# Constant matrix products in TensorE's waits at three stage borders

## The reference

```
xn     = rmsnorm(x) * (1 + sc1) + sh1;  proj = xn @ w_in
o_a    = rwkv7(proj[...])               # 8 heads, matrix state
o_b    = mamba2(proj[...])              # 16 heads, SSD state
merged = g_a * (o_a @ w_pa) + g_b * (o_b @ w_pb)
x      = x + gt1 * (merged @ w_out)
xn2    = rmsnorm(x) * (1 + sc2) + sh2
x      = x + gt2 * peer(xn2)            # product keys, top 16, 16384 experts
y      = rmsnorm(x) * (1 + scf) + shf
```

## Time and profile before

| | us |
|---|---|
| median of 3 runs | 4293.69 |
| lowest and highest | 4291.61, 4294.74 |
| the profiled execution | 4287.3 |
| its span, first to last instruction | 4285.7 |

### The profile page before, as it was taken

One profiled execution on the slowest core, in us unless ns is written; L12 is line 12 of the kernel. 1 busy time (PEld: TensorE's weight loads), 2 busy tenths in 40 slices (PEclk: granted clock), 3 DMA queues, 4 the chain that ended last, 5 costly groups with the idle time before them and its releaser, 6 DMA issues. The chain is left out here.

```text
span 4285.7 us, 85292 instructions
## 1 busy us (share of the span) xinstructions
PE 4061.5 (95%) x32204; PEld 3709.4 (87%) x32204; DVE 3228.8 (75%) x6232; ACT 1438.3 (34%) x2563; POOL 1309.1 (31%) x1006
## 2 busy tenths in 40 slices
PE   8999999998669979999999997999999999999998
PEld 5998888887539869788888887999999999999998
DVE  5721425444853358899998997999999999999998
ACT  4212222121653222233358883222222222222223
POOL 5333231000012200144443333344443443434441
PEclk9999999999879999999999998999999999999999
DMA  6764674564643311144435668999999999999995
GB/s 219 229 205 177 228 243 159 217 222 153 160 156 106 125 56 35 57 145 143 144 125 201 224 216 314 303 299 300 304 300 299 301 300 303 300 299 299 301 303 197
DMA packets 532589, 928.61 MB, mean 217 GB/s; under 512 B 286848, under 2 KB 355200, under 8 KB 524816
## 3 DMA queue, kind: packets, MB, share of 16 engines
q1 hardware_dynamic: 396512, 549.91, 39.7%
q0 software_dynamic: 81056, 346.96, 24.2%
q10 hardware_dynamic: 54816, 28.85, 2.4%
HBM read 786.05 MB, written 206.30 MB: 232 GB/s over the span
## 5 line engine op out<-in xcount | busy, mean ns | idle before, releaser
L3586 POOL DMA_INDIRECT ex_rows<-expert_rows,ex_here x512 | 589.9, 1152 | 951.0 <-DVE acc_tok L3826 860.1
L3826 DVE SCALAR_TENSOR_TENSOR acc_tok<-ex_rows,ex_wsp,acc_tok 128x1024 f32<-128x1024 f32 x512 | 633.6, 1278 | 0.0
L2852 PE MATMUL ex_psa<-x_dense_high,eg_u_high 128*128 128x288 f32 x2048 | 604.7, 295 | 6.6 <-DVEq L3940 6.5
L2852 PE MATMUL ex_psa<-x_dense_low,eg_u_high 128*128 128x288 f32 x2048 | 604.7, 295 | 0.0
L2852 PE MATMUL ex_psa<-x_dense_high,eg_u_low 128*128 128x288 f32 x2048 | 604.5, 295 | 0.0
L2944 POOL TENSOR_TENSOR eg_u_low<-eg_u,eg_u_high 128x1024 fp32r<-128x1024 f32 x130 | 328.2, 2525 | 743.0 <-ACT eg_u_high L2939 743.0
L3705 ACT ACTIVATE ex_w<-ex_psa 128x288 f32<-128x288 f32 x256 | 105.4, 412 | 1059.4 <-PE ex_psa L2852 1059.4
L3618 PE MATMUL ex_pso<-ex_w_high,ex_v_high 128*128 128x288 f32 x2048 | 442.2, 298 | 17.9 <-DVE acc L3808 14.4
L3618 PE MATMUL ex_pso<-ex_w_high,ex_v_low 128*128 128x288 f32 x2048 | 440.2, 297 | 0.0
L3618 PE MATMUL ex_pso<-ex_w_low,ex_v_high 128*128 128x288 f32 x2048 | 438.9, 296 | 0.0
L3808 DVE TENSOR_TENSOR acc<-ex_pso,acc 128x576 f32<-128x576 f32 x512 | 373.7, 750 | 44.4 <-PE ex_pso L3618 44.4
(11 more groups left out here) (539 smaller groups left out, 9046.4 us busy)
## 6 DMA issues: line engine op xcount, KB each, us to landing
eg_u<-in_u SPq DMA_DIRECT2D x256, 512.0 KB, 5.4
expert_rows<-in_v SPq DMA_DIRECT2D x128, 512.0 KB, 6.9
ex_v<-in_v SPq DMA_DIRECT2D x128, 512.0 KB, 6.2
weights<-wt_stage SPq DMA_DIRECT2D x36, 1024.0 KB, 4.9
ex_g<-weights SPq DMA_DIRECT2D x128, 288.0 KB, 6.7
expert_rows<-eg_act SPq DMA_DIRECT2D x256, 128.0 KB, 1.7
proj<-in_out POOLq DMA_DIRECT2D x50, 548.5 KB, 6.2
in_w<-in_w_in SPq DMA_DIRECT2D x50, 512.0 KB, 5.1
```

Source lines behind the costliest of these rows:

```text
L2852: yield nc.tensor.matmul(out[:, 0:b - a], w[:, kc, :], half[:, kc, a:b], start=n == 0, stop=n == len(passes) - 1)
L3586: pool.indirect_dma_start(rows[i][:, :], None, table, index(here[par][:, t, j:j + 1]), element_offset=ROW_RUNS[t][0]).then_inc(s_row[i], 16)
L3826: v.scalar_tensor_tensor(out=acc_tok[:, t, :], in0=rows[i][:, at:at + D], scalar=wsp[:, i:i + 1], in1=acc_tok[:, t, :], op0=ALU.mult, op1= ...
```

## The change

A new helper issues products of the matrix of ones with a column of ones, broadcast to the width wanted, into a PSUM bank that nobody reads at that time. It increments no semaphore. It is called in five places: at the end of the sample stage (12 products of 512 columns, behind a wait for the fourth s_cp), at the start of the merge (6 of 288), at its end (12 of 288), at the start of the scores behind the first scaled tile (10 of 512), and at the end of the spread (24 of 128, into the bank of iota).

```
+def keep_array_busy(k, bank, count, width=512):
+    for _ in range(count):
+        k.nc.tensor.matmul(bank[:, 0:width], k.ones[:, :], bc(k.ones[:, 0:1], [P, width]), start=True, stop=True)
...
                 states(6)
                 states(7)
+                pe.wait_ge(s_cp, NPAIR)
+                keep_array_busy(k, ps_ce3[:, 2, :], 12)
...
+                keep_array_busy(k, pf[1], 6, TOK_CHUNKS_BANKED[0][1])
                 for m in range(KC):
                     h = m % 2
...
                     mm = nc.tensor.matmul(pf[0][:, a:b], k.ones[:, :], total[:, a:b], start=True, stop=True)
                 mm.then_inc(s_sum, 1)
+                keep_array_busy(k, pf[1], 12, TOK_CHUNKS_BANKED[0][1])
...
             @block.tensor
             def _(pe):
+                pe.wait_ge(NR.sem, NR.done("scaled", 0))
+                keep_array_busy(k, flat(pss[:, :, :]), 10)
                 for i in range(NQ):
...
                 in_line(body)
+                keep_array_busy(k, iota, 24, NK)
```

## The result

The changed kernel took 4297.95 us, the median of 15 runs (4292.70 to 4304.20); the kernel before, beside it, 4291.39 us, also of 15 (4284.59 to 4298.84). That is 6.6 us more; the ratio is 1.0016 with a 95% interval of 1.0008 to 1.0023. The forecast was 4301.8, within 4297 to 4307, and +8.1 us: the time is inside the range, though only 1 us above its lower end, and the change costs time but less than the 0.2% that I had named as the bound. The absolute forecast stood on a median of three runs of the kernel before (4293.69); on the 4291.39 of the 15 it would have been 4299.5.

The account below looks back on a forecast made before the run. The prediction had TensorE busy for 95% of the span, with only 13 us of half clock at three borders in reach. Its terms, 5.4 + 0 + 2.5 + 0 + 0.2 = +8.1 us, gave 4301.8 us, range 4297 to 4307.

Parts of the forecast that it names:

- What a constant product costs: Every constant product: 4 cycles a column, so 512 columns take 0.853 us at full clock and 1.707 at half.
- A: End of the sample stage: 12 products of 512 outlast SyncE's drain; +5.4 us, bounds 4.4 and 6.1.
- E: End of the spread: 24 products of 128 end about when SyncE's drain does; +0.2 us (0 to 0.4).
- C: End of the merge: 12 products of 288 outlast ScalarE's drain; +2.5 us, bounds 2.2 and 3.2.
- That constant products lift the clock: At the start of a run the clock stays low for 4.7 us, within 3.9 to 5.9, then rises.
- third rival: Products of a constant do not lift the clock, to be seen in A: about +30 us, 4324; chance 0.05.
- B: Start of the merge: 6 products of 288 take 2.9 us inside TensorE's 3.3 us wait; cost 0.
- D: Start of the scores: 10 products of 512 delay the first real product, but VectorE's pace hides this; cost 0.
- The gains: Faster starts of merge, scores and expert loop are hidden by ob_rounded, VectorE's pace and transfers; gain 0.
- first rival: Slow starts at the borders were on the path, so gains of 6.5 us reach the end: 4295.3 us; chance 0.07.
- second rival: At the borders the barrier is passed while constant products still stream: 4293.7 us, no change; chance 0.06.
- The sum: Whole kernel: 5.4 + 0 + 2.5 + 0 + 0.2 = +8.1 us, for 4301.8 us.

Follow-up runs that it names:

- e3: Changed kernel with only B, D and E, without A and C: 4288.08 us, ratio 0.9992 to the kernel before.
- e7: Changed kernel with only B and D, enlarged to 24 products of 288 and 20 of 512: 4302.65 us, timed once.
- e10: Changed kernel with only B and D, at 12 products of 288 and 14 of 512: 4294.48 us, timed once.
- e1: Changed kernel with only A, the other four calls out: 4294.93 us against 4291.62 for the kernel before, ratio 1.0011.
- e4: Changed kernel with only A, doubled to 24 products of 512: 4304.46 us, ratio 1.0031 to the kernel before.
- e6: Changed kernel, same places and counts, both operands of the constant products read as F32R: 4289.94 us against 4290.54 for the kernel before, ratio 0.9998.
- e8: Kernel before plus nine products of 288 ahead of the merge's output product and seven ahead of the norm sum: 4287.32 us against 4290.54, ratio 0.9993.
- e9: As e8 but eight products ahead of the output product: 4282.10 us against 4290.56 for the kernel before, ratio 0.9984.
- e12: The kernel of e9 again, unaltered: 4282.69 us against 4290.89 for the kernel before, ratio 0.9981.
- e2: Changed kernel with only C, the other four calls out: 4291.15 us, ratio 1.0000 to the kernel before.

## Why the prediction was right, point by point

**What a constant product costs: right.** 0.86 us for 512 columns at full clock (A doubled), 0.23 for 128 (24 took 5.5 us in E; worked out: 0.24), 0.50 for 288 (12 took 6.03 us in C; worked out: 0.48). One of the two supports was loose: the 512-wide records of the earlier trace rows differ by 0.47 us, not by the 0.43 of half of 2 x 512 columns / 1.2 GHz. The norm sum carried the figure.

**That constant products lift the clock: right.** The third rival (they don't, +30 us) is refuted by the clock of 0.93 and 1.00 in A, and by the first group of the merge in e3, where nothing but B's products ran ahead of it. But the rise came later than my bounds: in A it came about 6.4 us after the start of the run (1270.26 to some 1276.7, from 5 us at 0.93), where I had taken 4.7 with 3.9 to 5.9. At other places it came sooner: 4.3 to 4.6 us after the start of B in e3, e7 and e10, and 3.5 to 3.6 after that of D in e3 and e7, but 6.1 in e10.

**A: the right mechanism, mis-sized.** Forecast +5.4 within 4.4 to 6.1, measured 6.65, 6.67 and, with A alone, 3.78. The term was off by 1.3 us in the changed kernel: 0.9 from the later rise, and 0.4 because 12 products take 10.6 us at full clock where I had 10.24. The bound below was missed because the clock at the start of the run is not fixed: at high clock TensorE's own last products also end a microsecond earlier, which I had left out. That the total fell into the range in spite of a term outside its bounds in all three profiles is in part luck.

**B: cost 0, right, with too small a reserve.** I had held 5.8 us for 2.5 too many. Alone, B took 5.3 us and the end of m = 0 stayed at 24.1: the slack is 3.3 of wait and 2.4 more. That the clock would fall again ahead of the w_pb tiles (about +1 us) did not happen: in the changed kernel it is 1.00 from 1285.6 to 1305.0, and the end of m = 0 stayed where it was.

**C: right.** +2.5 within 2.2 to 3.2, measured 2.22, 2.22 and 2.23.

**D: right.** Cost 0 at a first real product 9.7 us behind the barrier; the limit, which I had put at 1557, 14.3 behind the barrier, is 15.8: a tile without waits takes 1.5 us on TensorE (one starts at 1572.76 and the next at 1574.25 in e7), not 1.8.

**E: right.** +0.2 within 0 to 0.4, measured 0.

**The gains: right, all three hidden.** The end of m = 0 comes 24.1 us behind the barrier with the clock at 1.00 as with 0.50. That refutes the first rival (4295.3). The timed difference of +6.6 us is nearer to my +8.1 than to its +1.6, which lies outside the interval of 1.0008 to 1.0023 (3.4 to 9.9 us); as an absolute time, its 4295.3 is nearer to the 4297.95 than my 4301.8, since both stood on the median of three. What decides are the traces: no stage is shorter beyond the scatter, in the changed kernel and in e3. The Trainium skill (TensorE: Matmul & The Clock Gate, "Why this matters for your kernels") advises to leave no idle gaps between bursts of products. Read as a rule for the time of this kernel, it would have had the change pay. The runs show both halves of the matter: in the changed kernel the clock is 1.00 behind every border, and the time followed only in the two waits of the merge where TensorE is what the next step waits for.

**That the barrier is passed: refuted.** The second rival. The drain of 7.92 us and A doubled decide it. The same page of the Trainium skill ("What happens when you issue a matmul") lets the sequencer run ahead of the products; the trace agrees, since TensorE reaches its drain at 1277.4 with eight microseconds of products ahead, and it is the drain that waits.

**The sum.** The terms as measured are 6.65 + 2.2 = 8.9 us in the profiled execution, where I had 8.1, and 3.8 + 2.2 = 6.0 where A meets the high clock. The timed +6.6 lies between them. Which mix of the two the timed runs held was not measured. The sum also leaves out the pace of the merge's output product, which I had not foreseen: with its 2.2 to 2.6 us and the scatter of the other stages the profiled span grew by 9.3 us. What it was in the timed runs is not known, so the agreement of 6.6 with the terms is weaker evidence than the drains.

## What to carry to other kernels

Ask of a stretch at half clock first whether anything waits for its end: the three slow starts at borders were hidden altogether, while two waits inside a stage, ahead of a norm sum and of an output product, were worth 3.5 to 4 us. Fill such a wait with less than its length, and put nothing ahead of a barrier that outlasts the other engines, for there the last queued product counts. A start has a slack, the time of its last input less all the work from its first product on; up to there late is free, and beyond it each microsecond is paid.

## What the runs showed of the hardware

The merge's output product ran at three paces, 11.84, 12.00 and 12.16 us a tile, at clock 1.00 and constant over all eight tiles of an execution. The products of w_pa and w_pb ahead of it, 125.4 us for seven m, had one pace in every kernel. At 12.16 the product behind one of 512 columns starts 240 ns after it, at 12.00 234 and at 11.84 230; those behind one of 288 keep 131 to 134. Before had 11.84 and 12.00, the changed kernel 12.16 twice; e1 to e3 had 11.84; e4, e6, e8, e9, e10 and e12 had 12.00; e7 had 12.16. Up to 2.6 us of a difference between two single profiles can come from this alone. What sets it stays open.

The clock at which TensorE's last four records of states ran in the sample stage differed between executions, with the same instructions ahead of them: they lasted 2.57 or 2.58 us (half clock) in ten of the 14 profiles, 1.63 us (full) in e1, e3 and e6, and 2.42 in e2, where the clock fell within the run (records of 664, 846, 1057 and 1054 ns). What the constant products cost there changed by 2.9 us with it.
